# One expert's down product inside the next expert's gate and up product, and a fourth home for first weight parts

## What is computed

```python
x = x + jnp.einsum('blm,md->bld', y, lw['w_out'])
x = x + moe_ffn(rmsnorm(x, lw['norm_ffn_g']), ...)
# moe_ffn: each token takes 2 experts of one of 4 groups; for the tokens xi of expert e:
a, b = jnp.split(xi @ w_gu[e], 2, axis=-1)      # w_gu[e]: 1024 x 1024
y = (jax.nn.silu(a) * b) @ w_down[e]            # w_down[e]: 512 x 1024
# each y is scaled by its gate and added to its token's row
```

## Time and profile before

| | us |
|---|---|
| median of 3 runs | 862.53 (862.05 to 862.95) |
| the profiled execution | 862.31 |
| its span, first to last instruction | 860.6 |

### The profile page before, as it was taken

How to read it: one execution, slowest core, us unless ns; L and a number is a source line. 1 busy time by engine, 2 the same in 40 slices (tenths; PEclk the granted TensorE clock), 3 DMA queues, 4 the chain that set the end, 5 groups by cost and what they waited for, 6 DMA issues and landing times.

```text
span 860.6 us, 10187 instructions
## 1 busy us (share of the span) xinstructions
PE 733.6 (85%) x3636; PEld 383.0 (45%) x3636; DVE 205.5 (24%) x570; ACT 146.0 (17%) x352; POOL 188.3 (22%) x188
## 2 busy tenths in 40 slices
PE   3999999999998999769999997777787877777783
PEld 3788778887866545433333332222222222222220
DVE  4241101385869300730111010100100100100120
ACT  4122412106354411101000010000000000000000
POOL 7010000070300100013223323123123122132121
PEclk9999999999998999979999999999999999999998
DMA  9652643120530397459999999999999999999992
GB/s 311 130 154 62 194 143 108 42 75 1 179 117 1 141 424 319 163 197 411 414 406 411 412 406 410 411 415 409 412 417 405 416 413 408 416 416 409 414 417 76
DMA packets 77013, 247.04 MB, mean 287 GB/s; under 512 B 24952, under 2 KB 44303, under 8 KB 52363
## 3 DMA queue, kind: packets, MB, share of 16 engines
q1 hardware_dynamic: 63825, 231.48, 68.2%
q0 software_dynamic: 11776, 8.58, 4.5%
q10 hardware_dynamic: 1378, 6.54, 1.9%
HBM read 240.47 MB, written 24.92 MB: 308 GB/s over the span
## 4 chain that ended last, share of the span: by engine, by line
PE 45%; SPq 29%; DMA 16%; DVE 5%; issue 3%; ACT 1%; POOL 1%; ACTq 0%; POOLq 0%; DVEq 0%
PE bank L1099 41%; SPq L582 20%; SPq L589 9%; DMA reg_a<-in_exp_w_gu 6%; DMA reg_b<-in_exp_w_gu 6%; PE bank L1102 4%; DMA ffn_in<-reg_x 1%; DMA reg_x<-in_x_prompt 1%; DVE reg_a L1853 1%; DVE reg_y L2063 1%; ACT reg_y L1082 1%; DVE small L1813 1%; DVE reg_y L2071 0%; DVE reg_y L1860 0%; POOL small L687 0%
## 5 line engine op out<-in xcount | busy, mean ns | idle before, releaser
L1099 PE MATMUL bank<-reg_w,reg_y 128*64 128x512 f32 (+2 forms) x512 | 137.0, 572 | 16.7 <-DMA reg_w<-in_exp_w_gu 16.7
L1099 PE MATMUL bank<-reg_a,reg_y 128*64 128x512 f32 x528 | 122.8, 601 | 22.3 <-DMA reg_a<-in_exp_w_gu 16.6
L1099 PE MATMUL bank<-reg_b,reg_y 128*64 128x512 f32 x528 | 122.7, 599 | 21.3 <-DMA reg_b<-in_exp_w_gu 15.6
L2067 DVE TENSOR_TENSOR reg_y<-reg_y,bank 128x256 f32<-128x256 f32 x32 | 13.5, 421 | 417.5 <-ACT reg_y L1082 417.5
L1099 PEld LDWEIGHTS bank<-reg_w,reg_y 128*64 128x64 f32 (+2 forms) x512 | 45.3, 144 | 96.3 <-issue 53.5
L1099 PE MATMUL bank<-reg_b,reg_w 128*128 128x260 f32 x384 | 85.3, 383 | 0.0
L1099 PEld LDWEIGHTS bank<-reg_a,reg_y 128*64 128x64 f32 x528 | 34.4, 137 | 102.1 <-issue 49.8
L1099 PEld LDWEIGHTS bank<-reg_b,reg_y 128*64 128x64 f32 x528 | 34.7, 136 | 100.2 <-issue 57.6
L1099 PEld LDWEIGHTS bank<-reg_b,reg_w 128*128 128x128 f32 x384 | 72.7, 190 | 12.1 <-issue 1.1
L687 POOL TENSOR_TENSOR small<-small 128x1 f32<-128x1 f32 (+4 forms) x18 | 20.4, 1136 | 194.5 <-DVE small L1902 69.6
L757 POOL DMA_INDIRECT out_y_p<-reg_y,reg_h x16 | 25.3, 1581 | 166.3 <-ACT reg_y L1086 166.3
(11 more groups left out here) (343 smaller groups left out, 641.6 us busy)
## 6 DMA issues: line engine op xcount, KB each, us to landing
reg_a<-in_exp_w_gu SPq DMA_DIRECT2D x44, 1024.0 KB, 28.0
reg_b<-in_exp_w_gu SPq DMA_DIRECT2D x44, 1024.0 KB, 27.8
reg_w<-in_exp_w_gu SPq DMA_DIRECT2D x40, 1024.0 KB, 28.1
reg_a<-in_exp_w_down SPq DMA_DIRECT2D x22, 1024.0 KB, 28.1
reg_b<-in_exp_w_down SPq DMA_DIRECT2D x22, 1024.0 KB, 28.3
reg_h<-in_exp_w_down SPq DMA_DIRECT2D x20, 1024.0 KB, 28.0
reg_w<-in_w_in SPq DMA_DIRECT2D x9, 1024.0 KB, 10.7
reg_w<-in_w_out SPq DMA_DIRECT2D x2, 2048.0 KB, 11.2
```

The costliest lines, as they stand in the source:

```text
L1099: return eng.matmul(out, lhsT, rhs, start=start, stop=stop, skip_group_check=True)
L2067: tt(hid[b], silu[b], bank[2 + b][:, 256:512], ALU.mult).then_inc(S["hid_made"], 1)
```

## The change

Four things change together.

1. A fourth home for parts 0 and 1 alone: part 0 in tiles 0 and 1 of x1's region, part 1 in tiles 2 and 4 (two pieces of 4 KB per partition). Parts 0 and 1 of expert e now live in home e % 4, parts 2 and 3 and the down weights in home e % 3 as before. Parts 0 and 1 of expert 3 are loaded ahead of parts 2 and 3 of expert 2: part 0 when tiles 0 and 1 are stored, part 1 when tiles 4 and 2 are.
2. SP's order for e = 3 to 31 becomes: parts 0 and 1 of expert e + 1, parts 2 and 3 of expert e, the down halves of expert e. Every wait is still on PE's progress with expert e - 3.
3. PE's order: inside the gate and up product of expert e, the turn of `hid` of expert e - 1 stands after part 0 (chunk 2), its down product after part 1 (chunk 4), and the next expert's `turn_tokens` after part 2 (chunk 6). The gate table moves behind part 1 of expert 0. `slot_table` still stands ahead of expert 31, and so ahead of expert 30's turn and down product. ACT and DVE follow that order.
4. Semaphores are merged to make room: `x_loaded`, `x1_stored` and `ffn_in_stored` become one `x_moved` per tile (16 for the load, 16 for each store), and three that nobody waits for become `passed`.

The core of the diff:

```diff
+        gu_first = [[w[:, 0:2, :], w[:, 2:4, :]] for w in gu_w]
+        gu_first.append([x_in[:, 0:2, :], x_in[:, 2:5:2, :]])
...
+            def load_expert(e, j, first):
+
+                if j < N_EXP - 1:
+                    load_gu(e + 1, (j + 1) % 4, (0, 1), first + e - 2)
+                load_gu(e, j % 3, (2, 3), first + e - 2)
+                load_down(e, j % 3, first + e - 2)
...
             load_down(2, 2)
             eng.wait_ge(bank_full[bank_of["Y3.0"]], turn_of["Y3.0"] + 1)
-            load_gu(2, 2, parts=(0, 1))
+            load_gu(2, 2, (0, 1))
+            for part, tiles in ((0, (0, 1)), (1, (4, 2))):
+                eng.wait_ge(S["x1_ss"], 8 + part)
+                for i in tiles:
+                    eng.wait_ge(x_moved[i], 16 * 3)
+                load_gu(3, 3, (part,))
             eng.wait_ge(bank_full[bank_of["Y3.1"]], turn_of["Y3.1"] + 1)
-            load_gu(2, 2, parts=(2, 3))
+            load_gu(2, 2, (2, 3))
             load_experts(0)
...
-            def expert(n, b, g, loads, gathered):
-
+            def gate_up(n, b, g, loads, first, first_loads, gathered, between):
 
                 eng.wait_ge(S["xe_made"], n + 1)
                 for c in range(KC):
+                    if c in between:
+                        step, args = between[c]
+                        step(*args)
+                    if c == 6 and gathered is not None:
+                        turn_tokens(1 - b, gathered)
                     part, within = divmod(c, KC // GU_PARTS)
...
-                if gathered is not None:
-                    turn_tokens(1 - b, gathered)
+            def turn_hidden(n, b):
                 eng.wait_ge(S["hid_made"], n + 1)
...
+                def expert(e, i=0):
+
+                    n = N_EXP * r + 12 * i + e
+                    gate_up(n, e % 2, *homes(e, i), tokens_of(e + 1, i), {2: (turn_hidden, (n - 1, 1 - e % 2)), 4: (down, (n - 1, 1 - e % 2, (e - 1) % 3, loads_of(e - 1, i)))})
+
                 turn_tokens(0, 256 * r + 16)
-                gate_table()
-                with eng.Fori(0, N_EXP // 6) as i:
...
+                gate_up(N_EXP * r, 0, *homes(0), tokens_of(1), {4: (gate_table, ())})
+                with eng.Fori(0, 2) as i:
+                    for e in range(1, 13):
+                        expert(e, i)
+                for e in range(25, N_EXP):
                     if e == N_EXP - 1:
                         slot_table(r + 4)
...
+                    expert(e)
+                turn_hidden(N_EXP * r + N_EXP - 1, 1)
+                down(N_EXP * r + N_EXP - 1, 1, (N_EXP - 1) % 3, loads_of(N_EXP - 1))
...
             def expert(n, b, last):
+                hidden_turned(n - 1, 1 - b)
                 if not last:
                     copy_xe(n + 1, 1 - b)
-                eng.wait_ge(S["xt_turned"], n + 1)
-                eng.tensor_copy(hT[b], bank[4 + b][:, 0:256].rearrange("p (k s) -> p k s", k=2)).then_inc(S["hT_made"], 1)
+                gated(n, b)
```

More of the change, by code:

```diff
@@ L572, in _, with load_gu @@
             eng.dma_start(x1[:, 0:4, :], x_dram).then_inc(S["x_reloaded"], 16)
-            def load_gu(e, g, free=None, parts=range(GU_PARTS)):
+            def load_gu(e, g, parts, free=None):
                 width = KC // GU_PARTS
@@ L581, in load_gu @@
                     src = gu_dram[bass.ds(e, 1)].rearrange("e p s c n -> (e p) s c n")[:, lo // 4, lo % 4:lo % 4 + width, :]
-                    eng.dma_start(gu_w[g][:, lo:lo + width, :], src).then_inc(gu_loaded[g][part], 16)
+                    home = gu_first[g][part] if part < 2 else gu_w[g][:, lo:lo + width, :]
+                    eng.dma_start(home, src).then_inc(gu_loaded[g][part], 16)
             def load_down(e, g, free=None):
@@ L589, in load_down @@
                     eng.dma_start(down_w[g][:, half], src).then_inc(down_loaded[g][half], 16)
-            def load_experts(first):
[L593 to L600, removed]
+            def load_expert(e, j, first):
[3 more added lines that the diff above has]
+                load_down(e, j % 3, first + e - 2)
+            def load_experts(first):
+                load_expert(3, 3, first)
+                with eng.Fori(0, 2) as i:
+                    for j in range(4, 16):
+                        load_expert(12 * i + j, j, first)
+                for e in range(28, N_EXP):
+                    load_expert(e, e, first)
             eng.wait_ge(S["yn_sq"], NTILE)
@@ L606, in _ @@
             for e in range(2):
-                load_gu(e, e)
+                load_gu(e, e, range(GU_PARTS))
                 load_down(e, e)
@@ L623, in _ @@
                     for e in range(3):
-                        load_gu(e, e)
+                        load_gu(e, e, range(GU_PARTS))
                         load_down(e, e)
+                    load_gu(3, 3, (0, 1))
                     load_experts(N_EXP * r)
@@ L746, in _ @@
             rounds = eng.value_load(n_rounds[0:1, 0:1], min_val=1, max_val=ROUNDS)
-            eng.wait_ge(S["ffn_in_stored"], 16 * NTILE)
-            eng.wait_ge(S["x1_stored"], 16 * NTILE)
+            for i in range(NTILE):
+                eng.wait_ge(x_moved[i], 16 * 3)
             def gather(e):
@@ L1077, in _, with gated, rows_out @@
             eng.sem_inc(S["y_copied"], 2)
[L1079 removed]
+            def gated(e, n, b):
                 eng.wait_ge(S["gu_done"], n + 1)
                 eng.activation(silu[b], bank[2 + b][:, 0:256], ACT.Silu, scale=slot_scale[:, 1, bass.ds(e, 1)]).then_inc(S["silu_done"], 1)
+            def rows_out(e, n, b, reused=None):
                 eng.wait_ge(S["down_done"], n + 1)
@@ L1088, in _ @@
             with eng.Fori(0, rounds) as r:
+                n = N_EXP * r
                 eng.wait_ge(S["round_open"], r + 1)
                 eng.wait_ge(S["slot_gates_made"], r + 1)
-                for b in range(2):
-                    expert(b, N_EXP * r + b, b)
-                with eng.Fori(1, N_EXP // 2) as i:
-                    for b in range(2):
-                        expert(2 * i + b, N_EXP * r + 2 * i + b, b, 16 * N_EXP * r + 32 * i)
+                gated(0, n, 0)
+                for e in range(2):
+                    rows_out(e, n + e, e)
+                    gated(e + 1, n + e + 1, 1 - e)
+                with eng.Fori(1, N_EXP // 2 - 1) as i:
+                    for b in range(2):
+                        rows_out(2 * i + b, n + 2 * i + b, b, 16 * N_EXP * r + 32 * i)
+                        gated(2 * i + b + 1, n + 2 * i + b + 1, 1 - b)
+                rows_out(N_EXP - 2, n + N_EXP - 2, 0, 16 * N_EXP * r + 16 * (N_EXP - 2))
+                gated(N_EXP - 1, n + N_EXP - 1, 1)
+                rows_out(N_EXP - 1, n + N_EXP - 1, 1, 16 * N_EXP * r + 16 * (N_EXP - 2))
         @block.tensor
@@ L1523, in expert, with down @@
                 ins.then_inc(S["xt_turned"], 1)
+            def down(n, b, g, loads):
                 eng.wait_ge(S["hT_made"], n + 1)
```

60 lines of the change are left out of this document (33 added, 27 removed).

## The result

The changed kernel takes **869.75 us** (median of 13 runs, 866.23 to 872.85), the kernel before beside it 863.31 (13 runs, 862.05 to 866.16): ratio **1.0069** (95% interval 1.0057 to 1.0081), 6.0 us more (4.9 to 7.0). Forecast were 863.6 us and a range up to 866.2. The profiled execution of the changed kernel took 870.15 us with a span of 868.4; the one of before 862.31 with 860.6.

A forecast was written before the change was run, and what follows sets the result against it. Weight transfers at a fixed rate were taken to bound the expert stage after 377 us, plus PE's work behind the last landings. Terms -5.1 + 0.2 + 0.2 + 2.0 + 3.8 = +1.1 us gave 863.6 us, range 859.7 to 866.2.

The forecast's parts named there:

- PE's own stalls inside an expert are no such thing: Expert stage: PE's stalls inside an expert can't move the end, since transfers bound it; no cost counted.
- Nothing: Parts of the change worth no time: merged semaphores, PE waits removed beside full DMA engines, gathers behind later scatters.
- The end: Last experts: PE has 16.1 us of work between two part 3s where landings alone need 12.3; +3.8 us.
- rival that the end costs nothing: Last experts: PE isn't late, so 3.8 drops out, giving -2.7, 859.8 us; chance 0.15.
- Do they fit?: Before expert 0: expert 3's early loads fit the idle time, barely overlapping the last store to ffn_in; +0.2 us.
- rival of a collision: Before expert 0: part 1 of expert 3 collides with the last store; 2.5 instead of 0.2, 865.9 us; chance 0.08.
- The clock returns later: Rival, expert 0: parts 0 and 1 run at 1.2 GHz, down load at 392.0; sum +3.2, 865.7 us; chance 0.13.
- The hole: Behind expert 0: the first down load goes out at 389.9 instead of 386.49, leaving transfers idle; +2.0 us.
- Bytes moved forward: Before expert 0: two parts of expert 3, 2 x 1.049 MB, load while engines stand idle; -5.1 us.

The follow-up runs named there:

- kernel 2: The changed kernel with the slot table inside expert 31, behind expert 30's down product, and expert 30's `hid` copied ahead of the slots: 866.27 us.
- kernel 1: The changed kernel with the gate table ahead of expert 0 again: 868.37 us.
- kernel 9: The changed kernel with 16 extra unread products in PE's idle time ahead of the first tokens: 868.23 us.
- kernel 6: The new order of work on PE, ACT and DVE, with the three homes and loads of the kernel before: 867.29 us.
- kernel 12: The changed kernel with the edits of kernel 1, kernel 2, kernel 5, kernel 8 and kernel 9 together: 858.13 us.
- kernel 3: The changed kernel with 16 extra unread products behind the down product inside each of experts 25 to 30: 868.60 us.
- kernel 8: The changed kernel with parts 0 and 1 of expert e + 2 ahead of expert e's down halves in SP's list: 866.17 us.
- kernel 5: The changed kernel with part 1 of expert 3 loaded behind parts 2 and 3 of expert 2, once the last tile is stored: 868.99 us.
- kernel 7: The fourth home with the kernel before's order of work, plus kernel 5's later load of expert 3's part 1: 861.23 us.

## Why the prediction was wrong, point by point

**"PE's own stalls inside an expert are no such thing"** is the step that failed most in the profiled execution, and "Nothing" repeats it. I counted PE's idle time as a sum, and the sum hardly changed. But it moved into fewer and longer waits, and behind the longest of them the granted clock fell: 0.93 on average in a stretch where it had been 1.00. Inside the stage that is hidden beside full DMA engines, as I wrote. At its end it isn't: 1.46 us in part 2 of expert 30 and 1.5 in the parts and turns behind the slot table. The rivals had a later clock at the start, none at the end.

**"The end", +3.8,** was right in its mechanism and short in its size: measured +6.6. The slot wait, the unbroken chain behind it and its order are as described: 17.7 us from part 3 of expert 30 (833.01) to the end of expert 31's parts (850.72), forecast 16.1. Of the missing 1.6 the clock is 1.5, and so is the 1.46 ahead of it. The rival that the end costs nothing is out; kernel 2 shows that it could be had by moving the slot table.

**"Do they fit?", +0.2,** was a mis-sized term. I took the store as done when its traffic ended, and 4 GB/s from 354 on as proof. Its traffic was down to 8 GB/s by 353 to 354, but SP's wait ended at 355.1. Part 1 therefore ran ahead of and beside the last store (10.09 instead of 8.91 us), and the first tokens came at 373.93 instead of 372.40: 1.5 us. The gather's 0.65 is no traffic of part 1: nothing moved from 369 to 372 us. It does go with the early part 1: in all seven kernels that load it so, the store and the gather's first instruction on POOL take 12.0 us together, in the kernel before 10.2 (8.91 + 1.31); what that instruction waits for is open. The rival of a collision named the mechanism, but put its point at 356.5 and its price at 2.5. The Trainium skill (DMA: Bandwidth & Descriptors, Anatomy of one DMA) says of transfers on the GpSimd path that their fixed cost of about 2 us is mostly the receipt of the last write, heaviest towards HBM. This store was issued by ACT, and the 2 us between the end of its traffic and the semaphore are of that size.

**"The clock returns later"** came true, at a chance of 0.13. Parts 0 and 1 of expert 0 took 6.38 us. Together with the collision the first load went out 2.1 us late and the down load at 393.40, past the 390.5 I named and past the rival's 392.0. Gate table first (kernel 1) brings back half of the down load's delay, extra products (kernel 9) three quarters of it: the gap ahead of expert 0 is the same in kernel 9 (0.86 us against 0.87), so the gap alone doesn't keep the clock low; without extra products ahead of it, filling it (kernel 1) still helps.

**"The hole", +2.0:** measured 10 us x (1 - 283 / 411) = 3.1 by the window from 390 to 400. With the clock at the high level (kernel 9) the down load follows the first by 12.8 us, against 12.4 in my count; the change has 13.8.

**"Bytes moved forward", -5.1,** fits: from the first load on, -5.1 + 2.25 (379.61 against 377.36) + 3.1 + 0.9 (411 against 412 GB/s over 380 us) is +1.15, beside the measured +1.35 at part 2 of expert 30. The 0.9 rests on rates rounded to 1 GB/s. Counted in the packets of the traces, over the 144 loads ahead of the last six, a load of 1 MB took 2.668 us before and 2.667 in kernel 6, and 2.671 to 2.676 in the twelve kernels with the fourth home: 0.5 to 1.1 us in sum. So the price goes with the fourth home, for whose 4 KB pieces I took 0.2; whether it is the pieces, no run separates.

With the end's 6.6 the profiled executions give +7.75 by terms, beside +7.95 measured. Every term but the first was too small, and two things, the clock and a late semaphore, lie behind most of it. The range failed since I let the rivals be exclusive: the collision and the later clock are links of one chain (later tokens, later clock, later down load) and came together, and the end's own term was short on top of them.

## What to carry to other kernels

In a stage bound by transfers, PE's idle time is free as a sum, but not in any shape: look at the longest single wait that a new order leaves in front of a product, and at what runs at the low clock right after it where the stage ends. A load that waits for a store starts when the store's semaphore comes, not when its traffic stops (here 2 us later); and a gain in bytes only reaches the end if the last expert's chain of work isn't already longer than its landings.

## What the runs showed of the hardware that I had not expected

The clock within a stage went with how waits were spread. These windows of the changed kernel lie around one wait of 4.72 us:

```profile
664.70:669.40 4.70, 0.01 (x2) 0.00 (x0) 0.00 (x0) 0.69 (x1) 2.54 (x2) 0.87 1.01 424
669.50:672.90 3.40, 3.40 (x8) 0.69 (x8) 0.00 (x0) 0.00 (x0) 1.58 (x2) 0.50 1.03 395
```

The products after it run a whole stretch at 0.50, so the four products of a part take 3.68 us where they take 1.94 elsewhere. With waits of at most 1.0 us and about the same idle time in sum, the kernel before shows 1.00 over the same 380 us; kernel 12, with at most 2.4 us in one wait for weights, shows 0.97. The length of one wait doesn't settle it: after the same wait of 2.74 us for the slot table, the next part took 3.00 us in the change and 3.03 in kernel 6, but 1.94 in kernels 3, 8 and 9. The Trainium skill (TensorE: Matmul & The Clock Gate, HAM oscillation) describes a kernel whose every wait for data lets the clock fall; here it falls behind some of the long waits (2.7 and 4.7 us in the change) and behind none of the short ones of the kernel before.

A gather beside one 1 MB load took 4.16 us (kernels 5 and 7) instead of 3.01. A store of 512 KB took 10.09 us instead of 8.91 when three loads of 1 MB instead of two had been issued in the 4 us ahead of it.
